# A transformer layer in split float32: score products on 128 rows, GpSimd's small loads behind x, the residual scaled on VectorE

## The reference

```
o_a = dsa_attention(...)            # an indexer picks 128 keys per query, then softmax
o_b = chunk_rel_attention(...)      # softmax with a clipped relative bias
o_c = window_sink_attention(...)    # softmax in a window, with a sink and a T5 bias
o_d = stick_breaking_attention(...) # no softmax, strictly causal
y = sum(sigmoid(gate_i) * (o_i @ w_branch_i))
x = layer_norm(ALPHA * x + y @ w_out, ln_mix_g, ln_mix_b)
hg, hu = split(x @ w_ffn_in)
x = layer_norm(ALPHA * x + (silu(hg) * hu) @ w_ffn_out, ln_ffn_g, ln_ffn_b)
```

## Time and profile before

| what | value |
|---|---|
| median of three runs | 923.53 us (921.58 to 925.58) |
| profiled execution, its own time | 923.47 us |
| its span | 921.7 us |
| TensorE matmul busy | 892.2 us, 97% |
| TensorE weight load busy | 713.5 us, 77% |
| VectorE busy | 466.4 us, 51% |
| ScalarE busy | 340.3 us, 37% |
| GpSimd busy | 55.5 us, 6% |
| DMA, mean | 92 GB/s |

### The profile page before, as it was taken

The page is one execution under the profiler, slowest core; times in us unless marked ns, Lnnn a source line. Parts: engine busy times, 40 slices in busy tenths (PEclk is TensorE's granted clock), DMA queues, the critical chain, the costliest instruction groups (busy, mean ns, idle before and its releaser), DMA issues.

```text
span 921.7 us, 10388 instructions
## 1 busy us (share of the span) xinstructions
PE 892.2 (97%) x4079; PEld 713.5 (77%) x4079; DVE 466.4 (51%) x742; ACT 340.3 (37%) x503; POOL 55.5 (6%) x92
## 2 busy tenths in 40 slices
PE   7999999999999999999999968999999999999996
PEld 4978887877677777677888846888888888888884
DVE  4244597784647639645363496434443334322127
ACT  4344357664435453542232441332222223211112
POOL 8200000000000000000000072000000000000001
PEclk9999999999999999999999987999999999999998
DMA  6621221211113112111236113222222222222202
GB/s 228 253 91 50 89 92 46 81 57 46 58 43 108 67 47 92 61 76 53 100 115 236 46 46 137 91 92 92 91 95 105 112 97 91 92 92 92 97 40 92
DMA packets 14152, 85.02 MB, mean 92 GB/s; under 512 B 1680, under 2 KB 1940, under 8 KB 5280
## 3 DMA queue, kind: packets, MB, share of 16 engines
q1 hardware_dynamic: 11952, 77.34, 23.3%
q0 software_dynamic: 2016, 6.86, 2.1%
q10 hardware_dynamic: 144, 0.26, 0.1%
HBM read 82.33 MB, written 2.13 MB: 92 GB/s over the span
## 4 chain that ended last, share of the span: by engine, by line
PE 92%; DVE 6%; DMA 1%; ACT 0%; issue 0%; POOL 0%; SPq 0%; DVEq 0%; POOLq 0%
PE bank L1031 62%; PE bank L1186 16%; PE bank L1157 4%; PE bank L1115 2%; PE bank L1114 2%; DVE x_lo L963 2%; PE bank L1144 1%; PE bank L1131 1%; PE bank L1055 1%; DMA xraw<-in_xT 1%; DVE x1t L959 1%; PE bank L1103 1%; PE bank L1248 1%; DVE resid L924 1%; DVE result L998 0%; DVE w_lo L707 0%
## 5 line engine op out<-in xcount | busy, mean ns | idle before, releaser
L707 DVE TENSOR_TENSOR w_lo<-raw,w_hi 128x2048 fp32r<-128x2048 f32 x69 | 158.1, 2292 | 232.5 <-ACT w_hi L473 209.9
L1031 PE MATMUL bank<-x_hi,w_hi 128*128 128x512 f32 x720 | 184.7, 395 | 1.0 <-DVE y L712 0.5
L1031 PE MATMUL bank<-x_lo,w_hi 128*128 128x512 f32 x720 | 178.2, 389 | 0.0
L1031 PE MATMUL bank<-x_hi,w_lo 128*128 128x512 f32 x720 | 177.9, 389 | 0.0
L1031 PEld LDWEIGHTS bank<-x_lo,w_hi 128*128 128x128 f32 x720 | 135.2, 188 | 28.6
L1031 PEld LDWEIGHTS bank<-x_hi,w_lo 128*128 128x128 f32 x720 | 135.1, 188 | 28.1
L1031 PEld LDWEIGHTS bank<-x_hi,w_hi 128*128 128x128 f32 x720 | 132.9, 188 | 30.4 <-issue 3.8
L473 ACT ACTIVATE w_hi<-raw 128x2048 fp32r<-128x2048 f32 x48 | 92.0, 1916 | 122.3 <-PE bank L1186 94.9
L1186 PE MATMUL bank<-w_hi,h_lo 128*128 128x512 f32 x176 | 56.8, 389 | 0.0
L1186 PE MATMUL bank<-w_lo,h_hi 128*128 128x512 f32 x176 | 56.8, 389 | 0.0
L1186 PE MATMUL bank<-w_hi,h_hi 128*128 128x512 f32 x176 | 56.8, 389 | 0.0
(11 more groups left out here) (213 smaller groups left out, 1079.0 us busy)
## 6 DMA issues: line engine op xcount, KB each, us to landing
raw<-in_stream SPq DMA_DIRECT2D x69, 1024.0 KB, 4.8
resid<-in_x POOLq DMA_DIRECT2D x1, 2048.0 KB, 8.3
xraw<-in_xT SPq DMA_DIRECT2D x3, 512.0 KB, 8.3
out<-result SPq DMA_DIRECT2D x3, 512.0 KB, 2.6
bias_b<-bias_vectors POOLq DMA_DIRECT2D x1, 1024.0 KB, 8.9
bias_a<-bias_vectors POOLq DMA_DIRECT2D x1, 1024.0 KB, 11.5
ln_g<-in_g POOLq DMA_DIRECT2D x2, 512.0 KB, 7.9
ln_b<-in_b POOLq DMA_DIRECT2D x2, 512.0 KB, 8.9
```

The source lines that it names most:

```text
L707: dve.tensor_tensor(w_lo[:, s, :], raw[:, s, :], w_hi[:, s, :].bitcast(f32), ALU.subtract).then_inc(lo_ready, 1)
L1031: ins = pe.matmul(dst, lhs[a](k), rhs[b](k), start=n == 0, stop=n == n_all - 1)
```

## The change

There are three parts. Score products: VectorE writes the low part of k on the other 64 rows of `k_low` too, and the third product runs over all 128 rows (which adds low q by low k). Small loads: GpSimd makes its masks first, then waits for the last piece of x and for chunk 1, and only then issues its five small loads. Residual: gain and offset are given to `resid` by VectorE, two token tiles in each of the FFN pairs 0 and 1, behind `w_lo` of the next gate chunk; GpSimd only waits for it before it reloads `ln_g` and `ln_b`.

```diff
--- before.py
+++ after.py
@@ -365,11 +365,6 @@
 
         @block.gpsimd
         def _(pool):
-            pool.dma_start(t5_sb[:], t5T).then_inc(tables_loaded, 16)
-            pool.dma_start(rel_sb[:], relR).then_inc(tables_loaded, 16)
-            pool.dma_start(sink_bc[:], bass.AP(sinks.tensor, sinks.offset, [[0, P], [1, HEADS]])).then_inc(sink_loaded, 16)
-            pool.dma_start(g1_col[:], g1c).then_inc(cols_loaded, 16)
-            pool.dma_start(b1_col[:], b1c).then_inc(cols_loaded, 16)
             steps = [0]
 
             def step(ins):
@@ -394,6 +389,13 @@
             pool.affine_select(out=neg_tri[:], in_=neg_tri[:], compare_op=ALU.is_ge, fill=0.0, base=0,
                                pattern=[[-1, P]], channel_multiplier=1).then_inc(consts_ready, 1)
 
+            pool.wait_ge(x_loaded[-1], 16)
+            pool.wait_ge(raw_loaded[1], 16)
+            pool.dma_start(t5_sb[:], t5T).then_inc(tables_loaded, 16)
+            pool.dma_start(rel_sb[:], relR).then_inc(tables_loaded, 16)
+            pool.dma_start(sink_bc[:], bass.AP(sinks.tensor, sinks.offset, [[0, P], [1, HEADS]])).then_inc(sink_loaded, 16)
+            pool.dma_start(g1_col[:], g1c).then_inc(cols_loaded, 16)
+            pool.dma_start(b1_col[:], b1c).then_inc(cols_loaded, 16)
             pool.wait_ge(tables_loaded, 32)
             lo = -(SEQ - 1)
             for a, b, bucket in t5_ranges(lo, P):
@@ -440,11 +442,6 @@
 
             for tok in range(TOK):
                 root(0, tok)
-            pool.wait_ge(turned, KT)
-            for tok in range(TOK):
-                step(pool.tensor_tensor(resid[:, tok, :], resid[:, tok, :], ln_g[:], ALU.mult))
-                step_wait()
-                pool.tensor_tensor(resid[:, tok, :], resid[:, tok, :], ln_b[:], ALU.add).then_inc(x1_scaled, 1)
             pool.wait_ge(x1_scaled, TOK)
             pool.dma_start(ln_g[:], bass.AP(g2.tensor, g2.offset, [[0, P], [1, D_MODEL]])).then_inc(ln2_loaded, 16)
             pool.dma_start(ln_b[:], bass.AP(b2.tensor, b2.offset, [[0, P], [1, D_MODEL]])).then_inc(ln2_loaded, 16)
@@ -741,7 +738,8 @@
                 q_stack, k_stack, k_low = places[kind, n % 2]
                 dve.wait_ge(stack_hi_ready, n + 1)
                 dve.tensor_tensor(q_stack[others, :], q[rows, :], q_stack[rows, :].bitcast(f32), ALU.subtract)
-                dve.tensor_tensor(k_low[rows, :], k[rows, :], k_stack[rows, :].bitcast(f32), ALU.subtract).then_inc(stack_lo_ready, 1)
+                dve.tensor_tensor(k_low[rows, :], k[rows, :], k_stack[rows, :].bitcast(f32), ALU.subtract)
+                dve.tensor_tensor(k_low[others, :], k[rows, :], k_stack[rows, :].bitcast(f32), ALU.subtract).then_inc(stack_lo_ready, 1)
 
             def index_unit(n):
                 h = UNITS[n][1]
@@ -969,6 +967,9 @@
                     dve.scalar_tensor_tensor(swi[:, j, :], swi[:, j, :], 1.0, banks[4 * parity + j][:], ALU.add,
                                              ALU.mult).then_inc(gated, 1)
                 low(2 * p + (FIN0 + 2), FIN0 % 2)
+                if early:
+                    for tok in (2 * p, 2 * p + 1):
+                        scale_rows(tok)
                 for j in range(2):
                     dve.wait_ge(up_done, 2 * p + (j + 1))
                     dve.wait_ge(gated, 2 * p + (j + 1))
@@ -978,6 +979,15 @@
                     dve.wait_ge(h_hi_ready, 2 * p + (j + 1))
                     dve.tensor_tensor(h_lo[:, bass.ds(2 * p + j, 1), :], swi[:, j:j + 1, :],
                                       h_hi[:, bass.ds(2 * p + j, 1), :].bitcast(f32), ALU.subtract).then_inc(h_lo_ready, 1)
+
+            def scale_rows(tok):
+
+                if tok == 0:
+                    dve.wait_ge(turned, KT)
+                    dve.wait_ge(ln1_loaded, 32)
+                step(dve.tensor_tensor(resid[:, tok, :], resid[:, tok, :], ln_g[:], ALU.mult))
+                step_wait()
+                dve.tensor_tensor(resid[:, tok, :], resid[:, tok, :], ln_b[:], ALU.add).then_inc(x1_scaled, 1)
 
             ffn_pairs(dve, ffn_pair)
             for c in range(FOUT0, N_CHUNKS - 1):
@@ -1085,7 +1095,6 @@
 
             def unit_scores(n):
                 kind, h, _ = UNITS[n]
-                rows, _ = stack_rows(kind, h)
                 q_stack, k_stack, k_low = places[kind, n % 2]
                 pe.wait_ge(stack_lo_ready, n + 1)
                 if n and UNITS[n - 1][0] == "I":
@@ -1100,7 +1109,7 @@
                             keys, dst = slice(P * kb, P * (kb + 1)), score[b][:, col:col + width]
                             pe.matmul(dst, k_stack[:, keys], q_stack[:, q0:q0 + width], start=i == 0, stop=False,
                                       skip_group_check=True)
-                            pe.matmul(dst, k_low[rows, keys], q_stack[rows, q0:q0 + width], start=False, stop=False,
+                            pe.matmul(dst, k_low[:, keys], q_stack[:, q0:q0 + width], start=False, stop=False,
                                       skip_group_check=True)
                             ins = pe.matmul(score[b][:, col:col + P], ident_bf[:], not_causal[:], start=False, stop=True,
                                             skip_group_check=True)
@@ -1112,7 +1121,7 @@
                         b, col, k0, width = score_place(kind, r)
                         queries, dst = slice(P * r, P * (r + 1)), score[b][:, col:col + width]
                         pe.matmul(dst, q_stack[:, queries], k_stack[:, k0:k0 + width], start=True, stop=False)
-                        ins = pe.matmul(dst, q_stack[rows, queries], k_low[rows, k0:k0 + width], start=False, stop=True)
+                        ins = pe.matmul(dst, q_stack[:, queries], k_low[:, k0:k0 + width], start=False, stop=True)
                     ins.then_inc(scores_done, 1)
 
             def unit_stage2(n):
```

## The result

The changed kernel took 887.05 us (median of 4 runs, 886.68 to 887.8), the kernel before 923.55 beside it (921.58 to 925.58): a ratio of 0.960, 95% interval 0.959 to 0.962. The profiled execution of the changed kernel took 887.8 us, its span is 886.1, so the two profiles are 35.7 us apart. The forecast was 883.8, the range 879.2 to 894.0.

What follows compares the result with a forecast made beforehand. TensorE's stream was taken to bound the kernel (92% of the chain). Norm 13.7, scores 22.5 and start 3.5 sum to 39.7 us off 923.47, giving 883.8 us, range 879.2 to 894.0.

Steps and rivals of the forecast that it cites:

- the start of the products on x_lo: First norm: TensorE begins these 16 products at 546.70 as before; at 0.227 us each they end at 550.3.
- w_lo of the "up" chunk: Behind the first norm: VectorE finishes it at 549.5, 0.8 us ahead of TensorE's need at 550.3.
- seven long L963 and one short: First norm before the change: seven subtractions take about 2.83 us beside GpSimd, one after it takes 0.68.
- The rival that the norm keeps its length: First norm: something other than GpSimd slows L963, or w_lo comes late; 897.5 us, chance 0.04.
- The gross saving: Score products over all units: 128 rows in place of 64 save 24.8 us before added waits.
- the slack between the scaled probabilities and their transposes: Units C0 to C2 and A0: 0.4 to 0.5 us remains, so no cost taken; at most 2 us if wrong.
- The rival of VectorE as the bound in most units: Unit slots: up to 0.7 us in each of 12 more units, 8.4 us; 892.3 us, chance 0.10.
- the rival of unchanged scores: Score products don't speed up on 128 rows: 907.7 us, or 895 with half the gain; chance 0.08 together.
- ends of 0.5 and 6: Start: 6 us gained with no DMA stall, 0.5 if SyncE's own loads make the stall; 3.5 taken.
- the landing of x's third piece "near 8": Start: with small loads moved, this piece lands near 8 us instead of 11.43, first chunk done near 20.4.
- rate and issue as bad together only while the small loads run: Start, DMA: reason for taking 3.5 us; low rate (87 GB/s) and slow issue (2.33 us) coincide with GpSimd's small loads.
- the issue at 4.11: Start, SyncE's queue: took 2.33 us before; the forecast is wrong if it still takes 2 us.

Runs made afterwards that it cites:

- e3: Changed kernel with part 3 undone, GpSimd scaling `resid` right behind the last transposes again; 901.63 us.
- e4: Changed kernel with GpSimd scaling `resid`, but only when the last x_lo is done; 889.59 us.
- e7: Changed kernel with the second k_low subtraction replaced by zeros from seven memsets, products still on 128 rows; 884.35 us.
- e6: Changed kernel with score products back on 64 rows as in e1, but the second k_low subtraction kept; 909.78 us.
- e2: Changed kernel with part 2 undone, GpSimd's five small loads first in its queue again; 889.80 us.
- e9: Changed kernel with x's five loads issued from ScalarE's queue, the weights' five from SyncE's; 886.14 us.
- e1: Changed kernel with part 1 undone, third score product on 64 rows and no second k_low subtraction; 908.97 us.
- e11: Changed kernel with the edits of e7 and e9 together; 883.83 us, ratio 0.956 to the kernel before.
- e8: Changed kernel with 18 unused products on constants in TensorE's wait ahead of x's third piece; 885.93 us.
- e12: e11 with twelve products on constants ahead of x's third piece; 882.59 us, ratio 0.955 to the kernel before.
- e5: The changed kernel again, nothing altered, as a control; 887.11 us.
- e10: Changed kernel with SyncE's fourth and fifth pieces waiting for x's second and third, chunk 1 for x's fourth; 887.18 us.

## Why the prediction was right, and where not

**Part 3** was right in mechanism and near in size. Forecast were 13.7; the norm's piece gave 14.7 (28.02 less 13.35) against the kernel before. Two terms of the working were off and partly cancel. It kept the start of the products on x_lo where it was, 10.7 us behind the mark (the last transposes); that stretch held some seven products at half clock before and none in the changed kernel, where the start is 9.4 behind the mark, 1.35 sooner. And w_lo of the "up" chunk, which it had 0.8 us ahead of its use, ended last and cost 0.3. Against e3 the piece gave 13.7 (27.09 less 13.35), the forecast's figure by chance. The us between the kernel before and e3 lies at the end: VectorE's last x_lo ends 23.95 us behind the mark in both, and TensorE then takes 4.1 us to the "up" chunk before (granted clock 0.50) and 3.1 in e3 (0.68). The prediction counts seven long L963 and one short; there were six and two, which changes nothing in the sum, since that goes by the rows of TensorE. The scaling's eight instructions took 1.22 us each (1.3 forecast), and TensorE waited for nothing else in the pairs 0 and 1. The rival that the norm keeps its length is out by e3 and e4: with the same work on GpSimd 11 us later no x_lo was lengthened.

**Part 1** was forecast at 22.5 and gave 20.5 in the stretch. Two terms were mis-sized. The gross saving is 512.21 - 489.00 = 23.2 with e7, in which one wait of 0.9 belongs to the faster scores: 24.1, against 24.8. The lengths of the score products alone give 23.9: 4.3 in I, 4.4 in D, and 5.1 each in B, C and A, where the forecast had 4.4, 4.4, 5.3, 5.3 and 5.4. The waits are 0.7 + 0.7 (1.4 forecast), 1.1 for sp_lo (0.9) and 0.9 before A1, which was not counted: 3.4 against 2.3. The prediction looked at the slack between the scaled probabilities and their transposes. The slack that broke was one step further, between probsT on ScalarE and the next unit's scores, behind `gates` and VectorE's branch addition (e7). The rival of VectorE as the bound in most units is out by e6, where twenty subtractions cost 1.4 to 1.7 us (its time is 883.8 + 8.4 = 892.2, not 892.3); the rival of unchanged scores by B0's rows. With zeros in the other rows (e7) the products are as short as with the low parts there, so it is the number of rows that counts and not what they hold. Whether the price is for 64 rows as such or for each change between 64 and 128, no run separates; that the load of the 128-row product behind a 64-row one (197.02) also began only with its product speaks for the change.

**Part 2** was forecast at 3.5 with ends of 0.5 and 6. It gave 2.7 by the medians (e2), 1.7 by the means of the first column and 0.2 in the pair of profiles. The size lies within the ends, the mechanism was right only in part. The step that failed is the landing of x's third piece "near 8": ScalarE took it up at 10.46 and 10.56. The forecast took rate and issue as bad together only while the small loads run. The changed kernel shows that they stay bad without them (111 and 129 GB/s from 5 to 7 us, 1.69 us for the issue at 4.57). The sign that the forecast named, the issue at 4.11, did fall from 2.33 to 0.43, but it fell in e2 as well, where the small loads are early: it was no sign of their effect. In e9 a second queue removed the long issues, and the weights' third piece still landed at 9.03. The forecast also left out that TensorE is through with the pieces ahead of the third earlier when x's second piece is early (taken up at 5.55, 7.73 before): it waited 4.25 us in place of 3.03, and then ran eleven products at half clock in place of seven. That second piece was early in e2 too (5.67), so its delay in the kernel before is not put down to the small loads. What sets the rate from 5 to 7 us in SyncE's own loads was not settled.

**The sum.** 14.7 + 20.5 + 0.2 is 35.4 of the 35.7 us between the two profiles, against 39.7 forecast. The 4.3 missing (measured less forecast) are +1.0 in the norm, -2.0 in the scores and -3.3 at the start. The medians put the start at 2.7 and the total at 36.5. Single undoings by medians (21.9, 2.7, 14.6) add to 39.2, 2.7 too many. The table suggests why: e1's profile holds a norm 2.4 us longer through the clock, where the code is the changed kernel's. Whether that is so in most executions of e1, and not in its profiled one alone, is open. That the median of 887.05 lies 3.3 us above the forecast comes from the start and the scores, with the norm's us working the other way.

## What to carry to other kernels

Where the alternating matmuls of one stream use different numbers of rows, fill the short ones up, with zeros where nothing else is to be added: here the wide product cost what its neighbours cost, and seven memsets stood in for twenty subtractions. When a stream gets faster, follow every chain that ends in it one step past the first slack, to the bank or buffer that the next unit takes. For edits of 1 to 3 us read the stretch that the edit touches in several profiles, and not the medians or a single pair.

## What the runs showed of the hardware

- A product on 64 rows between products on 128 costs more than one on 128: 0.76 us for a pair of 512 columns against 0.46, 0.51 against 0.17 for 128 columns (B0 of the changed kernel: 189.21 to 189.38). Neither the weight load of the 64-row product (196.59) nor that of the next product on 128 rows (197.02) was hidden behind the product before it.
- VectorE and GpSimd lengthened each other where VectorE reads two operands of SBUF: six instructions of 0.68 us took 2.7 to 2.9 in e3, and two of 2.3 took 4.1 and 4.5 in e4. A product with one operand in a bank kept 0.67 us in e4.
- TensorE ran six or more products 0.427 us and not 0.227 apart behind its wait for x's third piece in every profile with nothing in that wait (2.75 to 6.0 us: before, changed, e1 to e7, e9 to e11) but e3's, where after 2.94 us of wait they were 0.23 apart at once. What decides wasn't found. With products on constants in the wait every product behind it kept the full clock (e8, e12, one profile each).
- The same instructions behind the first norm took 13.35 us or up to 15.8 in different profiles, with a granted clock in their first five us of 1.00 or of 0.50 to 0.71. 13.35 came with the full clock, 13.7 to 13.9 where the clock was back at 1.00 in the next five us (e5, e10, e12), 15.2 to 15.8 where it was not (e1, e4, e6). What sends it one way or the other wasn't found.
